# Requests for tiles of sums moved ahead of the shift stores, 32 late sums moved into layer 1's output projection, a third modulation buffer in the recurrence

## The chip, the cores and the metric

The kernel runs on one core of a Trainium2 chip. The metric is the time of one execution on the device, in microseconds (us). Before the change the median of three runs is 3972.62 us (3971.62 to 3973.78).

## What is computed

Two transformer blocks on 256 latent tokens and 256 context tokens, D = 2048, all in fp32. The first mixes an RWKV-7 recurrence (16 heads, two directions) with multi-head latent attention and has a gated feed-forward part (FFN) with a convolution; the second has two layers of pooling and differential attention. The change concerns the modulation vectors:

```python
# first block
sh1, sc1, g1, sh2, sc2, g2 = split(silu(c) @ w_ada + b_ada, 6)
h = rms_norm(x) * (1 + sc1) + sh1
... recurrence, attention, merge, w_out ...
x = x + g1 * rms_norm(out);  x = x + g2 * rms_norm(conv_ffn(...))
# second block, for layer l = 0, 1 (update_ctx only for l = 0)
shift, scale, gate = split(silu(c_2) @ w_ada_2[l] + b_ada_2[l], 3)
shift_c, scale_c, gate_c = split(silu(c_ctx_2) @ w_ada_2[l] + b_ada_2[l], 3)
h = rms_norm_2(x) * (1 + scale) + shift;  p = h @ w_in_2[l]
x = x + gate * (merge(...) @ w_out_2[l])
```

## The kernel before

**The chunks.** Every large product is cut into rounds of (mostly) 16 chunks. A chunk is 128 rows by 512 columns of a weight matrix. SyncE loads two chunks per DMA (512 KB) into `raw`, a ring of four pairs. ScalarE rounds a chunk to `whi` (line 1593), VectorE makes the rest `wlo` (`lo`, line 2238), and TensorE multiplies in three passes (line 891). `whi` and `wlo` have four slots, and VectorE runs three chunks ahead (`LA = 3`). The rounds come in this order: ckv, kpe, cq, mla, kv (4 rounds), r (2), lora, gl, the recurrence (8 iterations, in the code `rwkv`), gate (8), rproj (4 of 8 chunks), mproj (4), wout (4), the FFN (a first pass of 32 chunks, ten of 48, a last one of 16), and then for each layer l of the second block poolv (2), qkva (48 chunks), poolg (2), qkvb (48 chunks), attng (2) and out (4). The text writes qkva0 for l = 0 and qkva1 for l = 1 (the second block's second layer); "layer 1" of the second block in the change's name is l = 0, "layer 2" is l = 1. In layer 2 most chunks are multiplied with 256 columns of activations, those of keys and values with 512.

**The sums.** Part of the modulation is computed on VectorE, not on TensorE: 416 sums, each a product of a tile of the transposed weights (128 x 1024 values, 512 KB) with the condition vector, added up along the row (`reduced`, line 2254) and read from the accumulator. They stand between the chunks' `wlo`, spread by constants: `RED_KV` in each of kv's rounds 2 to 4, `RED_R` in r's, `RED_LORA`, `RED_GATE`, `RED_MPROJ`, `RED_WOUT`, `RED_FFN`, and `RED_VALUES`, `RED_A`, `RED_B`, `RED_C` in the second block. `red_done` counts them. Numbers 0 to 63 have a tile each, through three buffers `red_own`; 64 to 383 come in pairs, two sums to a tile, through two buffers; the last 32 (384 to 415) have a tile each again. These are half rows of the 16 blocks of layer 2's gate, and `RED_C` puts them into qkva1: 2, 20 and 10 in its three groups of 16 chunks.

**Pool's queue.** Pool (GpSimd) issues the tiles' DMAs and all other loads and stores that aren't weights, one after the other, with its waits in program order. `reduce_own(m0, m1)` asks for tiles m0 to m1 - 1 of the first 64, and waits for sum m - 3 before tile m; `reduce_in` (line 694) does so for the others. In kv's rounds 2 to 4, r's two and lora (the loop over `p_`, lines 718 to 738) Pool waits for each of four shifted blocks (`sh_done`), stores it, waits till all four stores have landed (`sh_st`), frees `sh_out` (`sh_free`), in the first pass stores `cond_keep` (2 MB), and then asks for the next tiles. DMAs of all queues share the same 16 DMA engines.

**The recurrence.** In each of its 8 iterations TensorE also multiplies one column tile of `w_ada` (16 x 128 rows by 512 columns) in 8 halves of 512 KB (`ada_half`, line 861, and `ada_mm`, line 857). They go through `ADA_RAW = 2` buffers `ada_raw`; `ada_used` counts the halves used, and Pool (line 700) asks for the next when its buffer is free. The first two of an iteration are asked for at the end of the one before. They stand in TensorE's program between the solves, the chunk steps (lines 1225 to 1229), the chunk outputs (1236 to 1241) and the first state steps (1338); VectorE makes `g1t` and `hd` (2658, 2659) from the chunk steps.

**The order around the late sums.** In the second block Pool reloads `cond_c` (1 MB, the condition vector) and the last 32 tiles in layer 2, after `pw` has landed; VectorE waits for `cond_c` at the start of qkva1 and for `red_done` 416 before the output projection of layer 2. In layer 1's output projection (`out_add`, line 3089) VectorE splits `mix` between the chunks of the first round; `cond_c` lies in `mix`.

**Other loads in Pool's queue.** `oT` (2 MB) is reloaded in the gate rounds (line 801), `x1` (2 MB, line 806) after the last split of `oT`, which is in rproj's last round. Before the change Pool comes to this load only after the request for the tile of sums 116 and 117, and this request waits for sum 113, which stands in mproj's first round.

## Time and profile before

| | before |
|---|---|
| median of 3 runs | 3972.62 us |
| profiled execution | 3977.09 us, span 3975.4 us |
| TensorE matmul busy | 3721.8 us (94%) |
| TensorE weight load busy | 3199.8 us (80%) |
| VectorE busy | 2688.7 us (68%) |
| ScalarE busy | 1724.4 us (43%) |
| DMA | 667.54 MB, mean 168 GB/s |
| mean granted TensorE clock | 0.975 of full speed |

How to read it: the page has the busy time of each engine, the chain of work that ended last, followed back from the last instruction, and the costliest groups of instructions. A busy share is an average over stages with different limits, so the rows below are taken stage by stage. In windows of the span the columns are: from and to, length, then for each engine its busy time and number of instructions, then the granted clock, the mean share of the 16 DMA engines and what they moved. PE is TensorE, PEld its weight load, DVE VectorE, ACT ScalarE, SP SyncE.

### The profile page before, as it was taken

Reading aid. Unit: us, or ns where it says so; the run is one execution under the profiler, and the core shown is the slowest. Engines: PE = TensorE matmul, PEld = TensorE weight load, DVE = VectorE, ACT = ScalarE, POOL = GpSimd, SP = SyncE. Lnnn points to the kernel's source line nnn. Section 1 sums busy time; section 2 is a strip of 40 time slices with the busy share of each in tenths; the row PEclk is TensorE's granted clock in tenths of the full one; section 3 lists DMA queues with packets and bytes.
Section 4 is the critical chain, followed back from the end, with each engine's and each line's share of the span. In section 5 each row is a group of like instructions: output and inputs, shape, how many; then the busy total and the mean of one; then the engine's idle time right before and its main releaser. Section 6 shows DMA issues by size and latency. Waiting matters only on the chain.

```text
span 3975.4 us, 84227 instructions
## 1 busy us (share of the span) xinstructions
PE 3721.8 (94%) x34998; PEld 3199.8 (80%) x34998; DVE 2688.7 (68%) x4743; ACT 1724.4 (43%) x3140; POOL 252.0 (6%) x441
## 2 busy tenths in 40 slices
PE   6999999788888999989999999899999999899999
PEld 2788778666666999989999999887777778777879
DVE  2544477766666786888888888767666643767375
ACT  2544323534344454455444444542433442524354
POOL 0000021111111000000000000000000000010000
PEclk7999999899999999999999999999999999999999
DMA  9422588231322786756777677545235133573336
GB/s 372 151 80 62 206 284 262 78 99 56 100 63 82 240 270 218 240 168 212 233 221 241 217 233 230 193 154 181 74 127 163 60 131 96 162 231 117 117 101 191
DMA packets 290011, 667.54 MB, mean 168 GB/s; under 512 B 21152, under 2 KB 31392, under 8 KB 287600
## 3 DMA queue, kind: packets, MB, share of 16 engines
q1 hardware_dynamic: 233392, 441.73, 34.6%
q0 software_dynamic: 56256, 220.58, 17.6%
q8 instruction: 275, 4.51, 0.5%
q14 instruction: 88, 0.72, 0.1%
HBM read 644.40 MB, written 17.83 MB: 167 GB/s over the span
## 4 chain that ended last, share of the span: by engine, by line
PE 73%; DVE 10%; DMA 9%; issue 4%; ACT 3%; SPq 0%; POOL 0%; POOLq 0%; DVEq 0%; ACTq 0%
PE psum L891 57%; DMA red_own<-in_w_adaT 2%; DVE wlo L2238 2%; PE psum L1153 2%; DMA red_a<-in_w_adaT 2%; DMA ada_head<-in_w_ada 1%; PE psum L1203 1%; DMA ada_raw<-in_w_ada 1%; PE psum L857 1%; PE psum L916 1%; ACT whi L1593 1%; DVE junk_l L2254 1%; DMA red_raw<-in_w_adaT 1%; PE psum L1084 1%; DVE smx L3038 1%
## 5 line engine op out<-in xcount | busy, mean ns | idle before, releaser
L1593 ACT ACTIVATE whi<-raw 128x512 fp32r<-128x512 f32 (+3 forms) x1568 | 970.7, 623 | 1469.3 <-PE psum L891 1425.9
L2238 DVE TENSOR_TENSOR wlo<-raw,whi 128x512 fp32r<-128x512 f32 (+3 forms) x1568 | 1042.2, 680 | 737.3 <-ACT whi L1593 726.5
L891 PE MATMUL psum<-hhi,whi 128*128 128x512 f32 (+1 forms) x2416 | 835.9, 346 | 55.9 <-DVE wlo L2238 27.2
L891 PE MATMUL psum<-hlo,whi 128*128 128x512 f32 (+1 forms) x2416 | 814.3, 337 | 0.0
L891 PE MATMUL psum<-hhi,wlo 128*128 128x512 f32 (+1 forms) x2416 | 814.1, 337 | 0.0
L891 PEld LDWEIGHTS psum<-hhi,whi 128*128 128x128 f32 x2416 | 462.9, 192 | 158.5 <-DVE wlo L2238 58.0
L891 PEld LDWEIGHTS psum<-hhi,wlo 128*128 128x128 f32 x2416 | 462.9, 192 | 48.1
L891 PEld LDWEIGHTS psum<-hlo,whi 128*128 128x128 f32 x2416 | 463.5, 192 | 46.5 <-issue 2.2
L891 PE MATMUL psum<-fhi,whi 128*128 128x256 f32 x1408 | 402.6, 286 | 12.9 <-DVE wlo L2238 8.3
L891 PE MATMUL psum<-flo,whi 128*128 128x256 f32 x1408 | 400.7, 285 | 0.0
L891 PE MATMUL psum<-fhi,wlo 128*128 128x256 f32 x1408 | 400.7, 285 | 0.0
L891 PEld LDWEIGHTS psum<-fhi,whi 128*128 128x128 f32 x1408 | 272.5, 194 | 16.4 <-DVE wlo L2238 11.5
L891 PEld LDWEIGHTS psum<-flo,whi 128*128 128x128 f32 x1408 | 272.7, 194 | 0.0
L891 PEld LDWEIGHTS psum<-fhi,wlo 128*128 128x128 f32 x1408 | 272.6, 194 | 0.0
L891 PE MATMUL psum<-uhi,whi 128*128 128x256 f32 x704 | 201.4, 286 | 2.8 <-DVE ulo L2836 2.8
L891 PE MATMUL psum<-ulo,whi 128*128 128x256 f32 x704 | 200.1, 284 | 0.0
L891 PE MATMUL psum<-uhi,wlo 128*128 128x256 f32 x704 | 200.1, 284 | 0.0
L891 PE MATMUL psum<-mixhi,whi 128*128 128x512 f32 (+1 forms) x512 | 174.3, 341 | 5.6 <-ACT stmp L2198 3.9
L891 PE MATMUL psum<-mixlo,whi 128*128 128x512 f32 (+1 forms) x512 | 172.8, 338 | 0.0
L891 PE MATMUL psum<-mixhi,wlo 128*128 128x512 f32 (+1 forms) x512 | 172.8, 337 | 0.0
L891 PEld LDWEIGHTS psum<-uhi,whi 128*128 128x128 f32 x704 | 136.2, 193 | 4.4 <-DVE ulo L2836 3.0
L2254 DVE CUSTOM_DVE_ANT_0 junk_l<-red_raw,cond_l,mod 128x1024 f32<-128x1024 f32 x106 | 134.6, 1280 | 7.5 <-DMA red_raw<-in_w_adaT 7.5
(459 smaller groups left out, 6950.2 us busy)
## 6 DMA issues: line engine op xcount, KB each, us to landing
raw<-in_w_in SPq DMA_DIRECT2D x328, 512.0 KB, 4.3
red_raw<-in_w_adaT POOLq DMA_DIRECT2D x115, 512.0 KB, 5.2
raw<-in_w_out SPq DMA_DIRECT2D x96, 512.0 KB, 3.8
raw<-in_w_gate SPq DMA_DIRECT2D x88, 512.0 KB, 5.1
raw<-in_w_val SPq DMA_DIRECT2D x88, 512.0 KB, 4.3
raw<-in_w_down SPq DMA_DIRECT2D x88, 512.0 KB, 5.3
ada_head<-in_w_ada SPq DMA_DIRECT2D x64, 512.0 KB, 10.3
red_own<-in_w_adaT POOLq DMA_DIRECT2D x64, 512.0 KB, 6.2
```

What stands on the lines that cost most here:

```text
L857: mm = pe.matmul(PS[4][t:t + 32, 0:256], sc[:, 2 * kh + kk, :], src[:, kk, nh * 256:nh * 256 + 256], start=(kh == 0), stop=(kh == 7), tile ...
L891: mm = pe.matmul(dst, l, r, start=(k == 0 and i == 0 and first), stop=(k == nch - 1 and i == 2), skip_group_check=True)
L916: pe.matmul(PS[bank][:, 0:src.shape[-1]], ones, src, start=(j == 0), stop=(j == of - 1)).then_inc(n_mm, 1)
L1084: done(pe.matmul(PS[5 + j % 2][:, :], lw2[0:LORA, j, :], (wl if j < 2 else al)[0:LORA, j % 2, :], start=True, stop=True), step)
L1153: return pe.matmul(PS[2 * d][HS[1 - e if l == 1 else e], ch(g)], aT[d][HS[1 - e], g, :], xinv[d][HS[1 - e], g, :], start=True, stop=True)
L1203: mx = pe.matmul(PS[2 * d][HS[1 - e], ch(g)], yinv[d][at_(e), g, :], bm[d][at_(e), g, :], start=True, stop=True)
L1593: act.activation(whi[:, lc % HL, 0:width], raw[:, (lc // 2) % RAW, lc % 2, 0:width], ACT.Copy).then_inc(w_hi, 1)
L2238: dve.tensor_tensor(wlo[:, lc % HL, 0:width], raw[:, (lc // 2) % RAW, lc % 2, 0:width], whi[:, lc % HL, 0:width].bitcast(F32), ALU.subtrac ...
L2254: dve.tensor_tensor_reduce(junk[n % len(junk)], (red_own[m % 3] if n < RED_OWN else raw_[m % 2])[:, :], cond[j][:, half], 1.0, acc if m % ...
L3038: own.then(dve.reduce_max(smx2[:, s:s + 2], psum[:, 4:6, 0:nk], axis=AX.X))
```

## The change

1. `reduce_own` asks for all tiles of the round's sums right after the fourth shift store is issued, ahead of the wait for the stores, of `sh_free` and, in the first pass, of the store of `cond_keep`. kv's rounds have 15 sums each for 16, lora 13 for 10.
2. `ADA_RAW` is 3. The third buffer lies at 60.5 KB, where `red_own`'s third buffer and `junk_1` lie. The waits are written for a number of buffers that doesn't divide 8.
3. The 32 last sums stand in rounds 2 to 4 of layer 1's output projection (`out0`), 11, 11 and 10, and use the buffers `red_raw`. Pool loads `cond_c` there, after `x2_in` and the last split of `mix`; VectorE waits for it before the second round. In layer 2 they are gone, with their waits; what reads the modulation of layer 2 waits for all sums.
4. rproj's rounds get one sum each, mproj's five for four, the FFN's ten passes 121 in all for 133, qkva0 12, 22 and 10 for 10, 20 and 10.

```diff
-ADA_RAW = 2
+ADA_RAW = 3
-RED_KV, RED_R, RED_LORA, RED_GATE, RED_MPROJ, RED_WOUT = 16, 3, 10, 7, 4, 8
+RED_KV, RED_R, RED_LORA, RED_GATE, RED_RPROJ, RED_MPROJ, RED_WOUT = 15, 3, 13, 7, 1, 5, 8
-RED_VALUES, RED_A, RED_B, RED_C = 8, (10, 20, 10), (21, 21, 0), (2, 20, 10)
+RED_VALUES, RED_A, RED_B, RED_C = 8, (12, 22, 10), (21, 21, 0), (0, 11, 11, 10)
...
-        ada_raw = [sb(f"ada_raw{i}", [P, 2, N], kb) for i, kb in enumerate((32, 36))]
+        ada_raw = [sb(f"ada_raw{i}", [P, 2, N], kb) for i, kb in enumerate((32, 36, 60.5))]
...
-                    pool.wait_ge(ada_used, 8 * ADA_PAIR * it + c - ADA_RAW + 1 + 8 * ADA_HEAD)
+                    before = c - ADA_RAW if c >= ADA_RAW else next(k for k in range(7, 0, -1) if k % ADA_RAW == c) - 8
+                    pool.wait_ge(ada_used, 8 * it + before + 1 + 8 * ADA_HEAD)
...
                         pool.dma_start(rkv[p_ * 4 - 16 + m, :, TOK:T2], sh_out[:, m, 0:TOK]).then_inc(sh_st[m], 16)
+                reduce_own(n_red, base + n)
+                n_red = max(n_red, base + n)
                 for m in range(4):
                     pool.wait_ge(sh_st[m], p_ * 16 + 16)
...
-            reduce_in(RED_EARLY + 4 + 2 * RED_GATE, RED_EARLY + 7 * RED_GATE + 4)
+            reduce_in(RED_EARLY + 4 + 2 * RED_GATE, RED_EARLY + 7 * RED_GATE + 3)
             pool.wait_ge(o_in, 16)
+            reduce_in(RED_EARLY + 7 * RED_GATE + 3, RED_EARLY + 7 * RED_GATE + 6)
...
-            reduce_in(RED_EARLY + 7 * RED_GATE + 4, RED_LATE)
+            reduce_in(RED_EARLY + 7 * RED_GATE + 6, RED_LATE)
...
-                else:
-                    pool.dma_start(cond_c[:, :], cond_keep[:, 0, :]).then_inc(cond_in3, 16)
-                    reduce_in(RED_BOTH, RED_ALL, red_a)
-                    pool.wait_ge(cond_in3, 48)
                 pool.wait_ge(at_dve[l], 2 * len(AT_DVE[l]))
                 if l == 0:
                     pool.dma_start(xall[:, :, :], x2_keep).then_inc(x2_in, 16)
                     pool.wait_ge(x2_in, 16)
+                    pool.wait_ge(s_lo, 24)
+                    pool.dma_start(cond_c[:, :], cond_keep[:, 0, :]).then_inc(cond_in3, 16)
+                    reduce_in(RED_BOTH, RED_ALL)
+                    pool.wait_ge(cond_in3, 48)
...
                     split_lo(oT, ohi, olo, (2 * it + j + 6) % 8, 2)
+                    if j:
+                        reduced(lo_reduced.n, both_of(cond_l), [junk_1[:, :]])
+                        lo_reduced.n += 1
...
                     c = C0[f"out{l}"] + it * 16
+                    if l == 0 and it == 1:
+                        dve.wait_ge(cond_in3, 48)
                     for i in range(13 + ahead):
...
                         lo(c, (LA + i,))
+                        for _ in range((i + 1) * RED_C[it] // 16 - i * RED_C[it] // 16 if l == 0 else 0):
+                            reduced(lo_reduced.n, [cond_c[:, :]], [junk_1[:, :]])
+                            lo_reduced.n += 1
```

## Rows read from the trace of the kernel before

**Rows 1.** The page: chain that ended last, by line; costliest groups, `whi` and `wlo`.

```profile
PE psum L891 57%; DMA red_own<-in_w_adaT 2%; DVE wlo L2238 2%; PE psum L1153 2%; DMA red_a<-in_w_adaT 2%; DMA ada_head<-in_w_ada 1%; PE psum L1203 1%; DMA ada_raw<-in_w_ada 1%; PE psum L857 1%; PE psum L916 1%; ACT whi L1593 1%; DVE junk_l L2254 1%; DMA red_raw<-in_w_adaT 1%; PE psum L1084 1%; DVE smx L3038 1%
...
L1593 ACT ACTIVATE whi<-raw 128x512 fp32r<-128x512 f32 (+3 forms) x1568 | 970.7, 623 | 1469.3 <-PE psum L891 1425.9
L2238 DVE TENSOR_TENSOR wlo<-raw,whi 128x512 fp32r<-128x512 f32 (+3 forms) x1568 | 1042.2, 680 | 737.3 <-ACT whi L1593 726.5
```

**Rows 2.** Windows: kv's rounds 2 to 4, r's two, out0's second.

```profile
451.35:509.65 58.30, 53.13 (x225) 42.86 (x223) 32.79 (x51) 22.78 (x31) 9.05 (x17) 0.97 0.80 281
509.65:559.10 49.45, 44.01 (x182) 34.88 (x183) 38.75 (x63) 9.16 (x16) 11.17 (x21) 0.97 0.82 273
559.10:605.95 46.85, 45.17 (x196) 36.10 (x195) 37.27 (x61) 12.84 (x21) 10.64 (x20) 1.00 0.88 293
605.95:632.45 26.50, 23.07 (x174) 21.50 (x173) 23.67 (x40) 11.22 (x19) 5.28 (x10) 1.00 0.88 300
632.45:655.50 23.05, 23.05 (x194) 23.05 (x194) 19.03 (x34) 11.14 (x20) 3.90 (x8) 1.00 0.87 284
...
3251.15:3295.35 44.20, 44.20 (x193) 35.73 (x192) 15.70 (x26) 12.19 (x20) 0.00 (x0) 1.00 0.32 95
```

**Rows 3.** Windows: qkva1's first 16 and last 32 chunks, qkvb1's last 32.

```profile
3462.15:3488.75 26.60, 26.60 (x211) 26.10 (x210) 22.44 (x44) 11.14 (x21) 0.53 (x1) 1.00 0.55 165
3488.75:3601.85 113.10, 99.67 (x428) 76.69 (x427) 72.26 (x124) 27.92 (x50) 15.33 (x29) 0.97 0.66 215
...
3701.50:3791.65 90.15, 90.15 (x411) 71.95 (x410) 33.46 (x57) 28.37 (x50) 0.00 (x0) 1.00 0.33 100
```

**Rows 4.** Waits in the recurrence, 720 to 1330: total us, times, longest.

```profile
PE psum L857 <- DMA ada_raw<-in_w_ada: 13.6, 18, 2.4
```

**Rows 5.** Timeline of POOL in kv's second and third rounds: start us, us, instruction.

```profile
471.63 0.54 POOL L725 DMA_DIRECT2D rkv<-sh_out  x1 [2.95 <-DVE sh_out L2431]
...
475.33 1.58 POOL L692 DMA_DIRECT2D red_own<-in_w_adaT  x3
...
549.11 1.57 POOL L692 DMA_DIRECT2D red_own<-in_w_adaT  x3 [5.54 <-DVE mod L2254]
```

**Rows 6.** Timeline of DVE there: sum 2 and sum 15.

```profile
485.22 1.28 DVE L2254 CUSTOM_DVE_ANT_0 junk_e<-red_own,cond_e,vec 128x1024 f32<-128x1024 f32 x1 [8.74 <-DMA red_own<-in_w_adaT]
...
519.22 1.28 DVE L2254 CUSTOM_DVE_ANT_0 junk_e<-red_own,cond_e,mod 128x1024 f32<-128x1024 f32 x1 [3.80 <-DMA red_own<-in_w_adaT]
```

**Rows 7.** Line 692, tiles asked for between 480 and 620.

```profile
DMA to landing us min/median/max: 3.6/6.3/8.2
```

**Rows 8.** Timeline of PE in the second iteration: an `ada_raw` half, the chunk step.

```profile
867.46 0.64 PE L857 MATMUL psum<-ada_raw,sc 128*32 128x256 f32 x8 [1.34 <-DMA ada_raw<-in_w_ada]
...
870.55 0.34 PE L1225 MATMUL psum<-b_tok,wu 64*64 64x64 f32 x8
```

**Rows 9.** Timeline of DVE in the same stretch.

```profile
868.47 0.69 DVE L2659 TENSOR_TENSOR hd<-psum,dec 128x512 f32<-128x512 f32 x1
...
872.73 0.69 DVE L2658 TENSOR_TENSOR g1t<-psum,con 128x512 f32<-128x512 f32 x1 [2.05 <-PE psum L1229]
```

**Rows 10.** Line 698 in qkva1, 3480 to 3600: who waited (us, times), landing.

```profile
  DVE junk L2254: 37.3, 25
...
DMA to landing us min/median/max: 3.7/4.6/7.0
```

**Rows 11.** Timeline of DVE in out0's first round: the last split of `mix`.

```profile
3246.68 1.22 DVE L2733 TENSOR_TENSOR mixlo<-mix,mixhi 128x1024 fp32r<-128x1024 f32 x1 [0.26 <-ACT mixhi L1942]
```

**Rows 12.** Timeline of POOL in mproj: the load of `x1`.

```profile
1552.17 1.18 POOL L806 DMA_DIRECT2D x<-in_xT  x1
```

**Rows 13.** Windows: mproj's second round, an FFN pass, qkva0's first 16 chunks.

```profile
1559.90:1588.35 28.45, 25.03 (x195) 24.62 (x194) 19.72 (x34) 10.83 (x17) 1.60 (x3) 0.94 0.78 254
...
2232.00:2306.00 74.00, 71.71 (x578) 70.80 (x576) 60.32 (x113) 34.59 (x61) 3.60 (x8) 0.98 0.71 223
...
2659.35:2710.00 50.65, 50.65 (x211) 39.27 (x210) 42.45 (x65) 12.39 (x20) 2.77 (x6) 1.00 0.45 138
```

More of the change, by code:

```diff
@@ L80 @@
 RED_FIRST = 8
-RED_KV, RED_R, RED_LORA, RED_GATE, RED_MPROJ, RED_WOUT = 16, 3, 10, 7, 4, 8
+RED_KV, RED_R, RED_LORA, RED_GATE, RED_RPROJ, RED_MPROJ, RED_WOUT = 15, 3, 13, 7, 1, 5, 8
 RED_EARLY = 3 * RED_KV + 2 * RED_R + RED_LORA
-RED_PROJ = RED_EARLY + 7 * RED_GATE + 4 * RED_MPROJ
+RED_PROJ = RED_EARLY + 7 * RED_GATE + 4 * RED_RPROJ + 4 * RED_MPROJ
 RED_MID = RED_PROJ + 4 * RED_WOUT
@@ L862, in ada_half @@
                 c = 8 * j + kh
-                pe.wait_ge(ada_in[c % ADA_RAW], (it * 8 * ADA_PAIR // ADA_RAW + c // ADA_RAW + 1) * 16)
+                pe.wait_ge(ada_in[c % ADA_RAW], (it * len(range(c % ADA_RAW, 8, ADA_RAW)) + c // ADA_RAW + 1) * 16)
                 if kh == 0:
@@ L2141, in heads @@
                             hi(c, range(48, 48 + LA))
-                        if it == 0 and i == 2:
-                            act.wait_ge(red_done, (RED_TURN, RED_ALL)[l])
+                        if l == 0 and it == 0 and i == 2:
+                            act.wait_ge(red_done, RED_TURN)
                         for m in range(4):
@@ L2770, in _ @@
                     lo(c, (i,))
-                    if i % 2:
+                    if i % 2 or i == 8:
                         reduced(lo_reduced.n, both_of(cond_l), [junk_1[:, :]])
@@ L2889, in _ @@
                 if l == 1:
-                    dve.wait_ge(red_done, RED_BOTH)
+                    dve.wait_ge(red_done, RED_ALL)
                 gains(mod2, 48 * l + 16, V("norm_2", 16 * l, 16))
@@ L2957, in late @@
                             reduced(lo_reduced.n, both_of(cond_a), [junk_1[:, :]], red_a)
-                        elif lo_reduced.n < RED_BOTH:
+                        else:
                             reduced(lo_reduced.n, [cond_b[:, :], cond_a[:, 1, :]], [junk_1[:, :]], red_b)
-                        else:
-                            reduced(lo_reduced.n, [cond_c[:, :]], [junk_1[:, :]], red_a)
                         lo_reduced.n += 1
@@ L2966, in heads @@
                     c = C0[f"qkv{'ab'[it]}{l}"]
-                    late_n = (RED_A, RED_B)[it] if l == 0 else (RED_C, (0, 0, 0))[it]
+                    late_n = (RED_A, RED_B)[it] if l == 0 else (0, 0, 0)
                     def ropes(bs):
@@ L2977, in ropes @@
                             done(TT(qk[:, b, TOK:T2], rope2[:, 0, :], rope2[:, 1, :], ALU.add), f"t{b}", it)
-                    if l != it:
-                        dve.wait_ge(cond_in3, 32 + 16 * l)
+                    if l == 0 and it:
+                        dve.wait_ge(cond_in3, 32)
                     for i in range(16):
@@ L3084, in _ @@
                 dve.wait_ge(sg_done, 16 * l + 16)
-                if l:
-                    dve.wait_ge(red_done, RED_ALL)
                 def out_add(it, ahead):
                     c = C0[f"out{l}"] + it * 16
+                    if l == 0 and it == 1:
+                        dve.wait_ge(cond_in3, 48)
                     for i in range(13 + ahead):
```

## The prediction

> **What bounds the kernel now.** I read the page first: 57% of the chain that ended last is line 891, the matmuls of the weight chunks [rows 1], and TensorE is busy for 94% of the span. So most of the kernel stands at TensorE's own pace, and the change can't move that. What it can move are stages in which something else sets the pace. To find them I cut the span where VectorE makes `wlo` of a round's first chunk (16 such instructions are one round of 16 chunks) and compared each round with a quiet one of the same shape. A quiet round over 512 columns takes 44.20 us (the window from 3251.15), over 256 columns 23.05 (from 632.45) [rows 2]. Against these, kv's second, third and fourth rounds take 58.30, 49.45 and 46.85 and r's first 26.50 [rows 2]: 181.10 us where 3 x 44.20 + 23.05 = 155.65 would do, 25.4 us too many. Layer 2's stage qkva1 takes 113.10 us for its last 32 chunks, its twin qkvb1, with the same matmuls and no sums, 90.15 [rows 3]. In the recurrence TensorE waits for `ada_raw` [rows 4]. These three places hold what the change can win. (The timed runs can tell a change from none from about 0.2%, 8 us, on.)
>
> **Part 1, tiles ahead of the shift stores.** In kv's second round Pool stores four shifted blocks (the last is issued at 471.63), waits till they have landed, issues the 2 MB store of `cond_keep`, and only then, from 475.33 on, asks for tiles 2 to 4 [rows 5]. VectorE sits idle for 8.74 us before sum 2, until 485.22 [rows 6]. With the change tile 2 is asked for right behind the store, at 471.63 + 0.54 = 472.2. Tiles here land 6.3 us after issue in the median, 3.6 at best [rows 7]; without the 2 MB store ahead of it I take 5, so sum 2 starts at about 477, 8 us earlier. From there the sums run at the tiles' pace: sum 2 at 485.22, sum 15 at 519.22 [rows 6], 34.0 / 13 = 2.6 us each. Sum 14, now the round's last, starts at 477 + 12 x 2.6 = 508. At TensorE's pace VectorE would be there at 451.35 + 44.2 + 2 x 2.76 + 0.7 = about 502 (2.76 is 44.2 / 16); it is 6 us late. Its lead is three chunks, 8.3 us, less the 1.3 us that a chunk's `whi` and `wlo` take [rows 1], so 7.0: nearly covered. The `cond_keep` store moves to about 503 and costs the tiles there: 2 MB is four tiles' worth of traffic, some 4 us. Lateness peaks at about 10 us, 3 of them uncovered. After that 15 sums in 44.2 us ask for 2.95 us each, slower than the 2.6 that the tiles can do, so it shrinks again.
> In the third and fourth rounds the wait for the stores goes (tiles are asked for only at 549.11, after 5.54 us without anything on Pool [rows 5]; the fourth round has a second such place): 5.25 + 2.65 us. r's first round has a trouble of its own, four shifts in eight chunks of 1.44 us, for which I leave 1.5 of its 3.45 us. Left over the ideal are 3 + 1.5, and about 3 for time at the lower clock (0.97 in two of the rounds [rows 2]) and small misses: 7.5. **Gain 25.4 - 7.5 = 18 us.** Ends: 10, if the tiles' pace rises to 2.9 us as TensorE runs faster; 24, if hardly anything stays.
> What waits behind the moved requests: Pool now sits in the tiles' waits until the round's sum 11 is done, and `sh_free`, which lets the next round's shifts write `sh_out`, comes only after that. That is at chunk 13 or so; the next shift comes at chunk 1 of the next round, over 8 us later: nothing. lora gets 13 sums for 10, each 1.28 us [rows 6]: 4 us more over 16 chunks, still fewer than kv's rounds hold: nothing.
>
> **Part 2, three buffers in the recurrence.** Each of 8 iterations takes the 8 halves of a tile through two buffers, all towards its end. A half can be asked for only once the one two before it is used. TensorE's matmuls wait 13.6 us in 18 places for this, 2.4 at most [rows 4], 1.7 us an iteration. With three buffers each half has the time of one more use as lead, and those stand about 2.5 us apart, so these waits go. What is late next? In the second iteration the half at 867.46 waited 1.34 us [rows 8]. Without this wait the chunk outputs behind it come 1.3 us earlier; the chunk step after them, which started at 870.55 [rows 8], needs `hd` of VectorE, ready at 868.47 + 0.69 = 869.16 [rows 9], so it can start 1.3 us earlier too; and VectorE's 2.05 us of waiting for this step, which ended at 872.73 [rows 9], shrink with it. This wait is passed on whole. The later and shorter ones fall partly into waits of the state steps for VectorE. I take two thirds of 13.6: **gain 9 us.** Ends: 3, if VectorE's chain takes the place, and 14, all of it. The third buffer lies where a buffer of the early sums and the scrap tile of the late ones lie, both unused then.
>
> **Part 3, the 32 late sums.** In qkva1's last 32 chunks 30 sums take a 512 KB tile each through two buffers: 113.10 us where the twin needs 90.15 [rows 3]. VectorE isn't full (72.26 of 113.10); it waits for tiles 25 times, 37.3 us in all [rows 10]. Without the sums these chunks take the twin's time: 22.95 less. The first 16 (26.60, against 23.05 for a quiet round) keep the pool windows and lose 2 sums. **I take 22.5**; ends 18 and 26.
> The sums go into the last three rounds of layer 1's output projection, 11, 11 and 10. Such a round has VectorE busy for 15.70 of 44.20 us [rows 2]; 11 x 1.3 = 14 more fit. Tiles: one each 4.0 us through two buffers, so that a tile may take 8.0 - 1.6 = 6.4 us to land before it paces VectorE. The traffic would be 95 GB/s [rows 2] + 11 x 0.524 MB / 44.2 us = 225 GB/s, near the 215 of qkva1 [rows 3], where tiles landed in 4.6 us in the median [rows 10]. VectorE's new wait for `cond_c`: it is asked for when the last split is done, 3246.68 + 1.22 = 3247.9 [rows 11], is 1 MB, and is there some 8 us later, 3256. VectorE comes to this wait when TensorE has ended the round, three chunks after 3251, at about 3259, and has added its four blocks. Behind it stand the chunks' `wlo`, with three chunks of lead. Nothing, or up to 3 us if the load comes late.
>
> **Part 4, the regrouping.** One sum now stands in each round of rproj. Pool therefore gets earlier through the tile that stood just ahead of the 2 MB load of `x1` at 1552.17 [rows 12]; this load then starts at about 1530, in rproj's last round, and without a tile beside it. The round in which it lay takes 28.45 us [rows 13] against 23.05. The contention with the weights moves there and is a fifth smaller: **gain 2**, ends 0 and 4. The FFN's ten passes get 121 sums for 133. Such a pass of 48 chunks would take 3 x 23.05 = 69.2; the worst takes 74.00 with clock 0.98 [rows 13], where weights and tiles land together. A tenth fewer tiles: **gain 1**, ends -4 and 6, since it may change which pass is hit. qkva0 gets 4 more sums: in its first 16 chunks VectorE has 42.45 us of 50.65 [rows 13], with two more 45: nothing, a loss of 2 us at most.
>
> **The sum.** 18 + 9 + 22.5 + 2 + 1 = 52.5 us. The profiled execution took 3977.1 (span 3975.4), 4.5 above the median of the runs: 3977.1 - 52.5 = 3924.6, and for the median 3972.6 - 52.5 = **3920**.
>
> **Rivals.**
> A. The early rounds are bound by the DMA engines, not by who asks when. For it: share 0.88 and 293 GB/s in the fourth round [rows 2]; in 44.2 us it needs 15 tiles, 8 chunk pairs and 4 stores, (23 x 0.524 + 1.05) MB / 44.2 us = 296 GB/s. Against: 300 GB/s in r's first round [rows 2], and the stalls follow a visible wait of Pool. The gain there would be 8 to 10: 3929. The Trainium skill, in "DMA: Bandwidth & Descriptors" (Specifications), puts a core's share of HBM at about 358 GB/s, which would leave room; no row here shows that much over such a round.
> B. In the recurrence VectorE's chain takes the waits' place and the gain is 0 to 3: 3928. For it: the state steps alternate between the two engines. Against: rows 8 and 9.
> C. Slower than before: the sums carry their price with them. If tiles land in 12 us in the output projection, a sum takes (12 + 1.6) / 2 = 6.8 us, 32 of them 218 us in 132.6: +85, against 52.5 won elsewhere: 4005. It begins at 6.4 us of landing and turns the sign at about 10. Against: 4.6 us at like traffic [rows 10].
> D. qkva1 is slow for its place, not for its sums; then 22.5 goes and 3943 stays. Against: its 25 waits for tiles [rows 10].
> On the price of a tile, a rule speaks against much gain from asking earlier: the Trainium skill, "DMA: Bandwidth & Descriptors" (Anatomy of one DMA), fits 2.0 us + bytes / 436 GB/s to a DMA of this queue, an estimate of 3.2 us for a tile, with which buffers would hardly run dry. The trace disagrees, with 6.3 us [rows 7], and decides.
>
> **How the numbers follow.** Forecast 0.70, A 0.11, B 0.12, C 0.02, D 0.05. The terms' ends reach from 24 to 74 us of gain; they won't all stand at one end, and I take 36 to 68. With A and B inside, 3904 to 3939 should hold 8 in 10. Faster 0.96, same 0.02, slower 0.02.
>
> **What would show it.** With windows cut as here: the four early rounds at 163 us together, VectorE's wait before sum 2 under 2 us; TensorE's waits for `ada_raw` near 0 and each iteration about 1.1 us shorter; qkva1's last 32 chunks at 90 to 91; the output projection still at 44.2 a round; mproj's second round near 24. Wrong, if tiles take over 8 us in the early rounds, if the recurrence keeps its period, or if a round of the output projection grows.

## The result, and the profile after

The changed kernel takes 3918.89 us (median of four runs, 3916.01 to 3922.04); the kernel before, run beside it, 3972.19 (3971.62 to 3973.78). The ratio is 0.9865, 95% interval 0.9848 to 0.9882: 53.3 us less, where 52.5 was forecast. The profiled execution took 3922.04 us (span 3920.4), so the two spans differ by 55.0 us.

First the page of the changed kernel, the lines that answer to [rows 1]. Weight matmuls are now line 895 (891 before), `whi` 1597, `wlo` 2242, the sums 2258, the early tiles' requests 692, the others' 698.

```profile
span 3920.4 us, 84227 instructions
...
PE psum L895 63%; DMA red_own<-in_w_adaT 2%; PE psum L1157 2%; DMA ada_head<-in_w_ada 1%; DVE wlo L2242 1%; PE psum L1207 1%; PE psum L861 1%; PE psum L920 1%; ACT whi L1597 1%; PE psum L1088 1%; DVE smx L3043 1%; PE psum L1222 1%; PE psum L998 1%; PE psum L982 1%; PE psum L983 1%
...
L2242 DVE TENSOR_TENSOR wlo<-raw,whi 128x512 fp32r<-128x512 f32 (+3 forms) x1568 | 1042.7, 680 | 730.6 <-ACT whi L1597 718.8
```

Line 895 now has 63% of the chain that ended last, up from 57% [rows 1]. The work itself hasn't changed: 84227 instructions, and VectorE's `wlo` takes 680 ns as before. Stages that were paced by something else are now paced by TensorE.

The windows of the changed kernel, cut at the same places as [rows 2], [rows 3] and [rows 13]: kv's rounds 2 to 4, r's two, mproj's second, out0's second to fourth, qkva1's first 16 and last 32 chunks, qkvb1's last 32. Columns as before.

```profile
451.10:500.85 49.75, 49.75 (x221) 41.22 (x220) 31.65 (x49) 20.86 (x28) 8.02 (x15) 1.00 0.78 268
500.85:551.15 50.30, 45.90 (x190) 35.93 (x189) 37.25 (x61) 11.53 (x19) 11.19 (x21) 0.97 0.89 309
551.15:594.20 43.05, 43.05 (x192) 35.66 (x191) 36.27 (x61) 11.93 (x21) 10.14 (x19) 1.00 0.89 305
594.20:620.85 26.65, 23.60 (x176) 21.95 (x175) 23.72 (x40) 11.72 (x19) 5.38 (x10) 1.00 0.88 302
620.85:643.90 23.05, 23.05 (x194) 23.05 (x193) 19.04 (x35) 11.14 (x20) 3.81 (x7) 1.00 0.87 284
1540.05:1562.75 22.70, 22.70 (x191) 22.59 (x190) 20.55 (x36) 10.65 (x17) 1.58 (x3) 1.00 0.78 247
3211.50:3255.75 44.25, 44.25 (x194) 35.73 (x193) 25.34 (x42) 12.21 (x20) 4.23 (x8) 1.00 0.69 228
3255.75:3301.80 46.05, 44.42 (x194) 35.75 (x193) 30.24 (x51) 12.20 (x20) 5.81 (x11) 1.00 0.68 216
3301.80:3347.25 45.45, 44.39 (x193) 35.72 (x192) 30.21 (x50) 12.20 (x20) 5.81 (x11) 1.00 0.65 209
3426.65:3453.15 26.50, 26.50 (x210) 26.08 (x210) 21.51 (x43) 11.13 (x20) 0.00 (x0) 1.00 0.50 148
3453.15:3545.05 91.90, 91.90 (x419) 73.49 (x418) 34.76 (x61) 27.27 (x49) 0.00 (x0) 1.00 0.33 103
3646.45:3736.65 90.20, 90.20 (x411) 72.02 (x410) 33.49 (x57) 28.56 (x50) 0.00 (x0) 1.00 0.32 99
```

The four early rounds (kv's second to fourth and r's first) take 169.75 us together, for 181.10. qkva1's last 32 chunks take 91.90 for 113.10 and now stand beside their twin's 90.20. out0's second round has kept its 44.2; the third and fourth have grown by 1.8 and 1.3, with clock 1.00 and TensorE idle for 1.6 and 1.1 us of them. This was not forecast.

Cut into stages in the same way, the span gives this (us; FFN includes the first half of the stage behind it, "layer 2 in" is qkva1 and the pool round behind it). The four single parts of the next section stand beside it. Each column is one profile:

| stage | before | after | part 1 | part 2 | part 3 | part 4 |
|---|---|---|---|---|---|---|
| early rounds | 181.1 | 169.7 | 173.1 | 181.6 | 181.6 | 179.5 |
| recurrence | 607.3 | 598.4 | 608.1 | 597.1 | 603.9 | 602.0 |
| rproj, mproj, wout | 242.8 | 237.6 | 241.1 | 239.9 | 239.7 | 237.6 |
| FFN | 880.0 | 866.5 | 877.7 | 881.0 | 879.6 | 870.1 |
| out0 | 178.7 | 181.9 | 178.7 | 178.7 | 181.4 | 178.8 |
| layer 2 in | 182.5 | 163.1 | 182.3 | 183.1 | 163.0 | 184.3 |
| median of the runs | 3972.2 | 3918.9 | 3967.6 | 3965.2 | 3956.5 | 3952.0 |

So the gains in the pair of profiles are 11.4 + 8.9 + 5.2 + 13.5 - 3.2 + 19.4 = 55.2 us, within 0.2 of the 55.0.

One pair of profiles doesn't give a stage's price well. Every run of the next section has a profile too, and in many of them the code of a stage is the same as before, or as in the changed kernel. These stand together here (us: lowest to highest, mean, in brackets the number of profiles):

| stage | code as before | code as in the change | difference of the means |
|---|---|---|---|
| early rounds | 179.5 to 181.6, 180.9 (4) | 166.1 to 169.7, 167.7 (4) | 13.2 |
| recurrence | 602.0 to 608.1, 605.3 (4) | 596.1 to 605.5, 599.6 (10) | 5.7 |
| rproj, mproj, wout | 239.7 to 242.8, 240.9 (4) | 237.6 to 239.1, 237.9 (10) | 3.0 |
| FFN | 877.7 to 881.0, 879.6 (4) | 864.6 to 870.1, 867.5 (6) | 12.0 |
| out0 | 178.7 to 178.8, 178.7 (4) | 181.4 to 183.0, 181.9 (7) | -3.1 |
| layer 2 in | 182.3 to 184.3, 183.0 (4) | 163.0 to 163.1, 163.0 (10) | 20.0 |

They add up to 50.8 us. So a gain read from the one pair of profiles is off by some 2 us in the early rounds, the merge (rproj, mproj, wout) and the FFN, and by some 3 in the recurrence.

### The profile page after: what moved, and what is told of

It reads as the page before. It is cut to its first block, busy times and chain, and to the rows that moved or that the text cites. A ratio compares the mean times of both kernels' runs of the same rounds, so it can differ in the third digit from the quotient of the medians.

```text
span 3920.4 us, 84227 instructions
## 1 busy us (share of the span) xinstructions
PE 3703.3 (94%) x34998; PEld 3192.7 (81%) x34998; DVE 2688.3 (69%) x4743; ACT 1723.9 (44%) x3140; POOL 251.9 (6%) x441
## 4 chain that ended last, share of the span: by engine, by line
PE 79%; DVE 10%; DMA 4%; issue 3%; ACT 3%; SPq 0%; POOL 0%; DVEq 0%; ACTq 0%; POOLq 0%
PE psum L895 63%; DMA red_own<-in_w_adaT 2%; PE psum L1157 2%; DMA ada_head<-in_w_ada 1%; DVE wlo L2242 1%; PE psum L1207 1%; PE psum L861 1%; PE psum L920 1%; ACT whi L1597 1%; PE psum L1088 1%; DVE smx L3043 1%; PE psum L1222 1%; PE psum L998 1%; PE psum L982 1%; PE psum L983 1%
## 5 line engine op out<-in xcount | busy, mean ns | idle before, releaser
L698 POOL DMA_DIRECT2D red_raw<-in_w_adaT x145 | 76.6, 529 | 1216.4 <-DVE mod L2258 1194.8
```

Source lines behind the costliest of these rows:

```text
L698: pool.dma_start(bufs[m % 2][:, :], A["w_adaT"][m // 2 * P:m // 2 * P + P, m % 2 * HALF:m % 2 * HALF + HALF]).then_inc(red_in[m % 2], 16)
```

## The experiments

**The four parts alone.** Each is the kernel before with one numbered part of the change. The edit of each is that part of the diff shown ahead of the prediction; for part 1 it is

```diff
+                reduce_own(n_red, base + n)
+                n_red = max(n_red, base + n)
                 for m in range(4):
                     pool.wait_ge(sh_st[m], p_ * 16 + 16)
```

with the counts of sums left at 16 a round.

> The kernel before with the requests for tiles moved ahead of the wait for the shift stores, and nothing else (kv's rounds keep 16 sums each, lora 10). Theory: the wait of Pool behind the stores is what the early rounds lose; the four rounds (kv 2 to 4 and r 1, 181.1 us together before) fall to 170 to 173 and the kernel to about 3962. Rival A (the DMA engines bound these rounds and the one sum less per round made the difference): they stay above 177, the kernel above 3968.

Measured: 3967.56 us, ratio 0.999 (0.9979 to 1.0002). Of the stages only the early rounds moved clearly, 181.1 to 173.1, 8.0 us. Asking earlier is worth less than half of the 18 us forecast for it as long as a round has 16 sums; with 15 (the change) it is 11.4.

Part 2 alone, the third buffer with its waits:

```diff
-ADA_RAW = 2
+ADA_RAW = 3
```

> The kernel before with three modulation buffers in the recurrence, and nothing else. Theory: the waits for the tiles go and two thirds of them are won: the recurrence falls by 9 us, the kernel to about 3963. Rival B (VectorE's chain takes their place, and what the changed kernel won there came with the other edits): 0 to 3 us.

Measured: 3965.23, ratio 0.9983 (0.9974 to 0.9993). The waits for `ada_raw` are gone. These windows hold the recurrence in before, after and part 2 alone:

```profile
718.70:1326.00 607.30, 506.23 (x14440) 394.01 (x14440) 408.42 (x716) 252.07 (x452) 85.59 (x132) 0.93 0.27 80
```

```profile
707.10:1305.50 598.40, 508.08 (x14440) 396.39 (x14439) 408.34 (x716) 252.04 (x452) 85.89 (x132) 0.92 0.27 81
```

```profile
719.10:1316.20 597.10, 502.82 (x14440) 391.74 (x14439) 408.24 (x717) 252.08 (x452) 85.90 (x132) 0.93 0.27 82
```

The same 14440 matmuls are busy for 506.2, 508.1 and 502.8 us, with clock 0.92 to 0.93: that part of the stage differs between profiles without any change to it. What the buffers change is the rest, in which TensorE isn't busy: 101.1, 90.3 and 94.3 us.

Part 3 alone, the 32 late sums, with the load of `cond_c` in layer 1:

```diff
-RED_VALUES, RED_A, RED_B, RED_C = 8, (10, 20, 10), (21, 21, 0), (2, 20, 10)
+RED_VALUES, RED_A, RED_B, RED_C = 8, (10, 20, 10), (21, 21, 0), (0, 11, 11, 10)
```

> The kernel before with the 32 late sums moved from qkva1 into the output projection of the second block's first layer, and nothing else. Theory: qkva1 with the stage behind it wins 19 to 20 us; rounds 3 and 4 of the output projection and the norm behind them lose about 4 as in the changed kernel, since a sum stands just ahead of the round's last blocks: the kernel at about 3957. Rival (the loss in the projection comes from tiles landing late because of what the other edits moved): the projection keeps 44.2 us a round and the kernel is at 3953.

Measured: 3956.5, ratio 0.9966 (0.9954 to 0.9978), 16.2 us. Layer 2's stage gives 19.5, the output projection takes 2.7 back (181.4 for 178.7), and the stage between them 0.9.

Part 4 alone, the regrouping:

```diff
-RED_KV, RED_R, RED_LORA, RED_GATE, RED_MPROJ, RED_WOUT = 16, 3, 10, 7, 4, 8
-RED_VALUES, RED_A, RED_B, RED_C = 8, (10, 20, 10), (21, 21, 0), (2, 20, 10)
+RED_KV, RED_R, RED_LORA, RED_GATE, RED_RPROJ, RED_MPROJ, RED_WOUT = 16, 3, 10, 7, 1, 5, 8
+RED_VALUES, RED_A, RED_B, RED_C = 8, (12, 22, 10), (21, 21, 0), (2, 20, 10)
```

> The kernel before with one sum in each round of rproj, five in mproj's, and so 121 for 133 in the FFN's ten passes and 4 more in qkva0, and nothing else (the early rounds keep their numbers). Theory: the FFN's passes lose time where a burst of three sums stands between chunks; with 12 sums a pass there are none and the ten passes fall from 706 to 695 us, mproj and wout by 5: the kernel at about 3956. Rival (the passes' stalls are accidents of phase, which any shift of time moves elsewhere): the passes stay at 700 or more and the kernel at 3963 or more.

Measured: 3952.02, ratio 0.9956 (0.9939 to 0.9972), 20.7 us by the medians; in its profile the stages of the merge give 5.2 and the FFN 9.9. The part for which 3 us were forecast is the largest of the four.

Beside these four the kernel before had a median of 3972.72 us. Their gains by the medians are 5.2 + 7.5 + 16.2 + 20.7 = 49.6 us, against 53.3 for all together: they add up within the scatter of such differences.

**The store of `cond_keep`.** On the changed kernel, the store goes from the loop's first pass (kv's second round) to its fifth, the end of r's second round. Pool then issues it at 638.34, so that its traffic lies in lora, which keeps its 40.3 us:

```diff
-                if p_ == 0:
+                if p_ == 4:
```

> The changed kernel with the 2 MB store of cond_keep issued in r's second round instead of kv's second. Theory: this store is what is left of the early loss, since it lands beside three tiles and the weights (they took 13 us instead of 6): the four early rounds fall from 169.8 to 162 to 165 us, lora loses at most 1, and the kernel is at about 3913. Rival A (the DMA engines' pace through all of kv's rounds): they stay at 168 or more and the kernel at 3918.

Measured: 3914.30 us (3905.52 to 3923.62), ratio 0.9848 (0.9824 to 0.9872). The early rounds take 165.5 us for 169.7, 4.2 less. But the size isn't settled by this pair: three later kernels with the same early rounds as the changed one took 166.1, 167.0 and 167.9, and the one other kernel with the store moved and 15 sums took 162.3 ("Together"). By the means, 163.9 for 167.7, the store costs 3.8, and the two groups are only 0.6 apart at their ends. What it does in the changed kernel is in the timeline. Pool, then VectorE, then TensorE:

```profile
503.04 0.53 POOL L692 DMA_DIRECT2D red_own<-in_w_adaT  x1 [1.27 <-DVE mod L2258]
503.70 0.54 POOL L736 DMA_DIRECT2D cond_keep<-cond_e  x1
504.85 0.53 POOL L692 DMA_DIRECT2D red_own<-in_w_adaT  x1 [0.61 <-DVE mod L2258]
```

```profile
511.13 1.29 DVE L2258 CUSTOM_DVE_ANT_0 junk_e<-red_own,cond_e,vec 128x1024 f32<-128x1024 f32 x1 [4.29 <-DMA red_own<-in_w_adaT]
...
518.45 1.29 DVE L2258 CUSTOM_DVE_ANT_0 junk_e<-red_own,cond_e,mod 128x1024 f32<-128x1024 f32 x1 [2.91 <-DMA red_own<-in_w_adaT]
```

```profile
513.09 0.50 PE L895 MATMUL psum<-hhi,whi 128*128 128x512 f32 x1 [2.90 <-DVE wlo L2242]
...
514.07 0.63 PE L895 MATMUL psum<-hhi,whi 128*128 128x512 f32 x1
514.50 0.63 PE L895 MATMUL psum<-hlo,whi 128*128 128x512 f32 x1
```

The tiles asked for on both sides of the store are late by 4.29 and 2.91 us for VectorE, the first of these stops TensorE for 2.90 us, and from 514.07 on its matmuls follow one another every 0.43 us, where it had been 0.23. The window shows the granted clock there, 0.50, the lower of the clock's two levels (1.2 for 2.4 GHz):

```profile
514.00:517.00 3.00, 3.00 (x8) 2.30 (x7) 1.47 (x3) 0.00 (x0) 0.55 (x1) 0.50 0.98 402
```

**The last sum of a round.** On the changed kernel, the sums of an output projection's round are spread over 15 chunks for 16, so that none stands behind the last chunk:

```diff
-for _ in range((i + 1) * RED_C[it] // 16 - i * RED_C[it] // 16 if l == 0 else 0):
+for _ in range(min(i + 1, 15) * RED_C[it] // 15 - min(i, 15) * RED_C[it] // 15 if l == 0 else 0):
```

> The changed kernel with the late sums of each output projection round spread over its first 15 chunks, none behind the last. Theory: the sum behind the last chunk delays VectorE's additions that free PSUM; without it rounds 3 and 4 fall from 46.0 and 45.5 to 44.2, the norm behind them from 51.7 to 50.7, the kernel to about 3915. Rival (the traffic of the tiles slows the projection): rounds 3 and 4 stay above 45.

Measured: 3916.16 us, ratio 0.9848 (0.9832 to 0.9865); the difference to the changed kernel is within the scatter of the medians, but the stage shows it: 179.1 us for 181.9, its rounds 44.2, 44.2 and 44.6. TensorE's waits in it, first in the changed kernel, then here (us in total, times, longest):

```profile
PE psum L895 <- DVE xall L3115: 2.7, 2, 1.6
```

```profile
PE psum L895 <- DVE xall L3115: 0.2, 1, 0.2
```

**The FFN's count and its bursts.** Undo only the FFN's and qkva0's part of the regrouping on the changed kernel:

```diff
-RED_VALUES, RED_A, RED_B, RED_C = 8, (12, 22, 10), (21, 21, 0), (0, 11, 11, 10)
+RED_VALUES, RED_A, RED_B, RED_C = 8, (10, 22, 0), (21, 21, 0), (0, 11, 11, 10)
```

The FFN gets what the second block doesn't: 133 sums.

> The changed kernel with 133 sums again in the FFN's ten passes and 12 fewer in qkva0 (10, 22 and 0), nothing else. Theory: the bursts of three sums come back and the ten passes go from 695 to 706 us, the kernel to 3929; the passes with 14 sums (the fourth, seventh and tenth) are the slowest. Rival (the gain there came from the sums' shift against the tiles' pairs, or from what lies ahead): the passes stay below 698, the kernel at 3919.

Measured: 3928.16 us, ratio 0.9886 (0.9869 to 0.9902), 9 us slower than the changed kernel by the medians. Its ten passes take 700.2 us for 695.1, with the ends 8.0 more. The theory had 706 for the passes, the rival less than 698: neither came true. With the same 133 sums in the same bursts the kernel before took 706.1 (705.9 to 708.7 in its four profiles). So the number of sums explains 5.0 of the 11.0 us; the other 6.0 came with other edits. Part 4 alone has 9.7 of the 11.0. Which edit it is, no run separates.

Why should a tenth fewer sums give even 5 us? In a pass two of the three groups of 16 chunks make sums, each in three bursts. With 121 sums all bursts but one are of two, with 133 thirteen are of three. The next kernel keeps the 133 and spreads them singly:

```diff
-                for i in range(4):
-                    lo(c, range(lc0 + 4 * i + LA, lc0 + 4 * i + 4 + LA))
-                    for _ in range((i + 1) * n // 3 - i * n // 3 if i < 3 else 0):
+                for i in range(16):
+                    lo(c, (lc0 + i + LA,))
+                    for _ in range((i - 2) * n // 12 - (i - 3) * n // 12 if 3 <= i < 15 else 0):
```

> The changed kernel with 133 sums in the FFN as in the run before this one on the FFN, but spread one by one over the chunks instead of in bursts of two and three. Bursts are the cause: the ten passes at 693 to 696 us. The number of sums is: 699 to 706.

Measured: 3921.02 us, ratio 0.9868 (0.9839 to 0.9897). The ten passes in before, after, with 133 sums, and with 133 spread. These windows run from TensorE's first matmul of the passes to its last, not from `wlo` to `wlo`, since in the spread kernel VectorE is ahead of TensorE by another amount:

```profile
1813.67:2517.96 704.29, 698.22 (x5762) 693.89 (x5760) 595.41 (x1107) 343.33 (x600) 34.35 (x65) 1.00 0.72 228
```

```profile
1786.36:2479.65 693.29, 693.29 (x5762) 691.66 (x5760) 582.70 (x1083) 342.75 (x600) 31.20 (x59) 1.00 0.72 227
```

```profile
1784.56:2482.84 698.28, 696.55 (x5761) 692.36 (x5760) 595.21 (x1107) 343.38 (x600) 34.52 (x65) 1.00 0.73 230
```

```profile
1782.32:2478.26 695.94, 694.09 (x5762) 691.86 (x5760) 597.21 (x1105) 341.29 (x600) 34.34 (x65) 1.00 0.74 231
```

The changed kernel's passes hold no idle time of TensorE at all. With the bursts taken apart, 133 sums take 695.94 us, 2.3 of the 5.0 us less, at the same traffic. (Cut at `wlo` it is 696.05 for 700.15, which makes it 4.1: more than TensorE gained.) TensorE's idle time is as long as with the bursts, 1.85 and 1.73 us; what is shorter is its matmuls' time. So about half of the count's 5.0 us goes with the bursts, by one profile of each, and the rest with the count. The worst pass of before [rows 13] shows what a burst of three does. Pool, VectorE, TensorE:

```profile
2248.50 0.53 POOL L698 DMA_DIRECT2D red_raw<-in_w_adaT  x1 [4.29 <-DVE mod L2254]
```

```profile
2251.43 1.28 DVE L2254 CUSTOM_DVE_ANT_0 junk_l<-red_raw,cond_l,vec 128x1024 f32<-128x1024 f32 x1
2252.63 1.28 DVE L2254 CUSTOM_DVE_ANT_0 junk_l<-red_raw,cond_l,vec 128x1024 f32<-128x1024 f32 x1
2255.92 1.28 DVE L2254 CUSTOM_DVE_ANT_0 junk_l<-red_raw,cond_l,mod 128x1024 f32<-128x1024 f32 x1 [1.99 <-DMA red_raw<-in_w_adaT]
```

```profile
2257.87 0.39 PE L891 MATMUL psum<-fhi,whi 128*128 128x256 f32 x1 [2.06 <-DVE wlo L2238]
```

The third sum needs a new tile. Pool could ask for it only at 2248.50, when the burst before had freed its buffer; it landed in 7.4 us, VectorE waited 1.99, and the next `wlo` stands behind this sum. Of the 6.0 us that TensorE waits for `wlo` in the ten passes of before, 5.5 are four such places, each right behind a third sum that had waited 0.64 to 1.99 us for its tile. They lie in the third, fourth, seventh and tenth pass; with 133 sums on the changed kernel there are two stops behind a sum's wait for its tile, of 0.40 us (a second sum, in the fourth pass) and 1.18 (a third, in the seventh). The tiles landed in 5.0 us in the median before and in 4.6 there; what made them faster isn't shown.

**What bounds the early rounds.** What keeps the early rounds of the kernel with the store moved, 165.5 and 162.3 us in its two profiles, from less? Two kernels on top of it. In the first the tiles of sums 0 to 63 are loaded by half and read twice (these sums are then not the reference's; all other work is in place):

```diff
-pool.dma_start(red_own[m % 3][:, :], A["w_adaT"][m // 2 * P:m // 2 * P + P, m % 2 * HALF:m % 2 * HALF + HALF]).then_inc(own_in[m % 3], 16)
+pool.dma_start(red_own[m % 3][:, 0:HALF // 2], A["w_adaT"][m // 2 * P:m // 2 * P + P, m % 2 * HALF:m % 2 * HALF + HALF // 2]).then_inc(own_in[m % 3], 16)
...
+twice = red_own[m % 3][:, 0:HALF // 2].unsqueeze(1).to_broadcast([P, 2, HALF // 2])
```

> The kernel with the later store, and the first 64 tiles loaded as half tiles (256 KB) that VectorE reads twice, so that its work stays and their traffic is halved; the 64 sums are not the reference's sums. Rival A, as it stands after the later store (what is left over the ideal in the early rounds, 10 us of 165.5, is the DMA engines' pace): the four rounds fall to about 158, VectorE's waits for these tiles to near 0. Other theory (VectorE's own order of shifts and sums): they stay at 162 to 166. r's first round keeps about 25.5 in both.

In the second the traffic of a tile stays, and a round has one sum less; lora takes the three:

```diff
-RED_KV, RED_R, RED_LORA, RED_GATE, RED_RPROJ, RED_MPROJ, RED_WOUT = 15, 3, 13, 7, 1, 5, 8
+RED_KV, RED_R, RED_LORA, RED_GATE, RED_RPROJ, RED_MPROJ, RED_WOUT = 14, 3, 16, 7, 1, 5, 8
```

> The kernel with the later store, kv's rounds with 14 sums each and lora with 16. If the tiles' pace is what is left: kv's three rounds lose 2 to 4 us more than with 15, lora stays at 40.3, the four early rounds at 161 to 163. If VectorE's order is: 165 as with 15.

Measured: 3914.58 us, 0.9852 (0.9823 to 0.9881), and 3916.41, 0.9857 (0.9827 to 0.9886). The windows over the four early rounds: before, after, store moved, half tiles, 14 sums:

```profile
451.35:632.45 181.10, 165.37 (x773) 135.34 (x772) 132.48 (x212) 56.00 (x84) 36.15 (x68) 0.98 0.84 285
```

```profile
451.10:620.85 169.75, 162.31 (x773) 134.76 (x772) 128.88 (x206) 56.03 (x84) 34.72 (x65) 0.99 0.86 295
```

```profile
450.75:616.30 165.55, 159.91 (x773) 133.82 (x772) 128.87 (x206) 56.05 (x84) 34.32 (x64) 1.00 0.85 289
```

```profile
451.50:609.90 158.40, 157.99 (x773) 133.88 (x772) 128.98 (x207) 56.04 (x84) 34.52 (x64) 1.00 0.69 221
```

```profile
453.60:611.95 158.35, 157.94 (x773) 133.88 (x772) 125.51 (x200) 56.04 (x84) 32.59 (x61) 1.00 0.85 292
```

Both reach the same floor, 158.4 us, in which TensorE is busy but for 0.4 us. The kernel with 14 sums reaches it at 292 GB/s, so the DMA engines carry the load (its tiles landed in 6.6 us in the median, as with 15). A round of kv has room for 14 tiles of that landing time, and not for 15: none of the six profiles with 15 whole tiles reached the floor. With the floor known, each kernel's excess splits in two: time in which TensorE stands still, and time that its 773 matmuls take beyond 157.9 us because the granted clock has dropped. Before: 15.7 + 7.5. After: 7.4 + 4.4. With the store moved: 5.6 + 2.0.

**Together.** First the store moved, the 15 chunks and 119 sums in the FFN:

```diff
-RED_VALUES, RED_A, RED_B, RED_C = 8, (12, 22, 10), (21, 21, 0), (0, 11, 11, 10)
+RED_VALUES, RED_A, RED_B, RED_C = 8, (13, 23, 10), (21, 21, 0), (0, 11, 11, 10)
...
-                if p_ == 0:
+                if p_ == 4:
```

> The changed kernel with the store in r's second round, no sum behind a projection round's last chunk, and 119 sums in the FFN (11 in the first pass, 12 in the others) with qkva0 at 13, 23 and 10. Theory: 6 + 4 + 1 us less than the changed kernel: about 3908. Rival A and the traffic theory: 3916 or more.

Measured: 3915.77 us, ratio 0.9851 (0.9834 to 0.9867). The stages are short (out0 179.4, FFN's ten passes 693.9, early 162.3, where the store's move alone had given 165.5), but the recurrence took 600.9 us, 4.8 more than with the store moved alone, and the median isn't distinguishable from the changed kernel's. Then 14 sums in kv's rounds and 16 in lora as well:

```diff
-RED_KV, RED_R, RED_LORA, RED_GATE, RED_RPROJ, RED_MPROJ, RED_WOUT = 15, 3, 13, 7, 1, 5, 8
+RED_KV, RED_R, RED_LORA, RED_GATE, RED_RPROJ, RED_MPROJ, RED_WOUT = 14, 3, 16, 7, 1, 5, 8
```

> All edits that won in a stage, on the changed kernel: the store of cond_keep in kv's last pass, 14 sums in each of kv's rounds and 16 in lora (the run before it reached 158.4 us in the four early rounds), the output projection's sums over 15 chunks, and 119 sums in the FFN with 4 more in the second block's first stage. Theory (the stages add up, and the rest of a run's time is TensorE's time at the lower clock): early rounds 158 to 160, output projection 179 to 180 for 181.9, FFN's ten passes 693.9 for 695.1, so 11 + 2.5 + 1 = 14 to 15 us less than the changed kernel at the same clock: median 3902 to 3910, ratio 0.983. Rival (what is won early is given back in the recurrence as time at the lower clock, since TensorE idles less before it): the recurrence takes 603 to 606 as in the run before, with TensorE's busy time in it 509 to 511 for 508.1, its idle time still 91 to 95, and the median stays at 3913 to 3918.

Measured: 3906.50 us (3905.45 to 3913.80), ratio 0.9845 (0.9831 to 0.9858), 63.6 us less than before on the same chip, where the change has 53.3. The interval overlaps the changed kernel's, so it is probably, not certainly, the fastest here. Its profiled execution took 3912.29 us, 5.8 above the median: early 158.4, out0 179.0, ten passes 693.9, and the recurrence 602.8:

```profile
697.66:1300.48 602.82, 509.62 (x14440) 397.54 (x14439) 408.40 (x717) 252.10 (x452) 85.92 (x132) 0.92 0.27 81
```

The idle time in it is 93.2 us, as in the others with three buffers; the matmuls take 509.6. The median is in the first theory's range. In this one profile the recurrence has come near the rival's numbers, 4.4 us longer than in the changed kernel's; the early rounds' 11.4, the output projection's 2.9 and the FFN's 1.2 are there all the same.

## Why the prediction was right, and where its steps were off

The median came within 1.1 us of the forecast, but the sum held by luck: by the stages of the pair the terms were 11.4, 8.9, 16.2 and 18.7 us (55.2 in all) for 18, 9, 22.5 and 3. By the means over all profiles they are 13.2, 5.7, 16.9 and 15.0 (50.8).

**Part 1: 18 us forecast, 11.4 measured (13.2 by the means).** The place and the first step hold. Tile 2 was asked for at 471.89 (forecast 472.2), landed in 6.2 us (taken as 5), and the wait before sum 2 fell from 8.74 [rows 6] to 1.92 us:

```profile
471.89 0.54 POOL L692 DMA_DIRECT2D red_own<-in_w_adaT  x1
```

```profile
478.14 1.28 DVE L2258 CUSTOM_DVE_ANT_0 junk_e<-red_own,cond_e,vec 128x1024 f32<-128x1024 f32 x1 [1.92 <-DMA red_own<-in_w_adaT]
```

What failed is "from there the sums run at the tiles' pace: 2.6 us each". From sum 2 to sum 15 they took 518.45 - 478.14 = 40.3 us, 3.1 each. With the store moved away it was 2.8 in one profile and 2.6 in the other, so the pace of [rows 6] was not wrong in itself: it doesn't hold across the store. The second step that failed is the price of the moved store: four tiles' worth of traffic, 3 us of it uncovered, for 4.2 measured in the pair and 3.8 by the means. The third is that the rest, which was to shrink again behind the store, stayed: with the store moved the early rounds are still 3.9 to 7.2 us above the floor. A tile that takes 6.3 us to land [rows 7] and 1.3 to be read comes through three buffers every 2.5 us if nothing else holds it up; against 44.2 / 15 = 2.95 that looked like room, but the runs reach the floor at 44.2 / 14 = 3.16 and not at 2.95. The lower end of the term, 10, had been reckoned for just this case, and nearly came true. The ideal of 155.65 us was 2.7 too low as well: the floor is 158.4.

What was said to wait behind the moved requests, `sh_free` and the next shifts, costs nothing: the kernels with 14 sums and with half tiles keep that order and reach the floor. lora takes 40.3 us with 10, 13 and 16 sums (40.4 in the last kernel).

**Rival A** had two halves. "Bound by the DMA engines" falls with 14 sums at 292 GB/s and the floor. But its number, a gain of 8 to 10, is near the 11.4, and what kept the early rounds off the floor once the store was moved is the pace at which tiles come: half the bytes a tile takes it away, with VectorE's work left as it was, and so does one tile less a round. The landing of the early tiles asked for between 480 and 600, first in the changed kernel, then with half tiles:

```profile
DMA to landing us min/median/max: 4.3/6.3/13.5
```

```profile
DMA to landing us min/median/max: 2.9/3.7/5.5
```

The Trainium skill ("DMA: Bandwidth & Descriptors", Anatomy of one DMA) fits 2.0 us + bytes / 436 GB/s to one DMA of this queue, an estimate of 3.2 us for a whole and 2.6 for half a tile. At 221 GB/s in the rounds the median is 1.1 us above this fit, at 295 GB/s 3.1 above. The fit has no term for other traffic; here the measured landing decides.

**Part 2: 9 us forecast, 8.9 in the pair of profiles, and that agreement is partly luck.** All 13.6 us of waits are gone [rows 4]. But by idle time, which the clock doesn't touch, the four profiles with two buffers have 97.5 to 101.1 us (mean 99.0) and the ten with three have 90.3 to 94.6 (mean 92.7): 6.3 us, 45% of the waits (14.2 in the mean of the four) and not two thirds. In the recurrence of the pair the idle time fell by 10.8 and the busy time grew by 1.9. What takes back the rest is in part VectorE, as rival B had it. In the means over the same profiles the waits for `ada_raw` fall by 13.9 us, those for VectorE's `zs` and `hd` grow by 3.8, and time for which the profile names nothing ("issue") by 3.2, which stays unexplained. In the pair these two rows have grown, the first from 12.3 us, the second from nothing:

```profile
PE psum L1342 <- DVE zs L2678: 13.9, 25, 0.7
...
PE psum L1229 <- DVE hd L2663: 2.0, 5, 0.4
```

**Part 3: 22.5 us forecast, 16.2 measured.** Rival D is out: without its sums qkva1 runs like its twin, 91.90 and 90.20 us. The term was mis-sized in two places. First, the 22.95 us were the difference of two windows that begin and end where VectorE makes a `wlo`. Such a mark runs ahead of TensorE or behind, and 1.8 us that the shorter window had given up came back in the pool round behind it (44.6 for 42.8). A stage should be cut where both kernels have caught up; then it is 19.4. Second, the output projection: the tiles landed in 4.7 us in the median (taken 4.6), `cond_c` in 5.4, and VectorE didn't wait for it. Rival C is out. The wait that did come is another. Sum 394 stood behind the round's last chunk and ahead of the four blocks' additions, which set PSUM free:

```profile
3262.43 1.28 DVE L2258 CUSTOM_DVE_ANT_0 junk<-red_raw,cond_c,vec 128x1024 f32<-128x1024 f32 x1 [0.54 <-DMA red_raw<-in_w_adaT]
3263.64 0.08 DVE L2258 DVE_READ_ACCUMULATOR2_ANT mod<- 128x1 f32 x1
3263.64 0.48 DVE L3114 SCALAR_TENSOR_TENSOR xall<-psum,mod,xall 128x256 f32<-128x256 f32 x1
3264.15 0.48 DVE L3115 SCALAR_TENSOR_TENSOR xall<-psum,mod,xall 128x256 f32<-128x256 f32 x1
```

```profile
3264.78 0.47 PE L895 MATMUL psum<-mixhi,whi 128*128 128x512 f32 x1 [1.63 <-DVE xall L3115]
```

TensorE's next round waits until the first additions have read its block. The prediction had asked what the new wait for `cond_c` holds up, and counted VectorE's busy time, but not what stands behind the last sum in its order. The kernel without a last sum takes 2.8 of the 3.2 us back.

**Part 4: 3 us forecast, 18.7 by the stages of the pair (15.0 by the means), and both of its steps failed.** Of the merge, 5.2 us for 2 in the pair, outside the end of 4; by the means it is 3.0, inside. mproj's second round, 28.45 us in [rows 13], took 25.3 to 26.7 in the three other profiles in which its code is the same. The load of `x1` went to 1519.04, where Pool has no other tile on its way, as forecast, though TensorE had by then begun mproj's first round (at 1518.84) and not rproj's last:

```profile
1508.72 0.53 POOL L698 DMA_DIRECT2D red_raw<-in_w_adaT  x1 [22.25 <-DVE mod L2258]
1519.04 1.18 POOL L810 DMA_DIRECT2D x<-in_xT  x1 [9.79 <-DVE olo L2737]
1530.76 0.54 POOL L698 DMA_DIRECT2D red_raw<-in_w_adaT  x1 [10.54 <-DVE mod L2258]
```

mproj's second round fell from 28.45 us to 22.70. The first grew from 24.3 to 25.5 by the `wlo` marks, but from TensorE's first matmul of it to the first of the next round it takes 23.1 us in every profile, the kernel before too. So the contention didn't move with four fifths of its price: TensorE no longer lost anything to it. That it had been the load and a tile together is argued, not shown: the load itself landed in 15.1 us before and in 11.4 after. Of the FFN, 13.5 us for 1, where the end was 6. "A tenth fewer tiles" reckoned with bytes. Of the ten passes' 11.0 us, 5.0 come back with the 133 sums, some half of them by the bursts; what gives the other 6.0 stays open. The prediction had reckoned the quiet pass at 69.2 us, but priced the worst [rows 13] by its share of traffic and didn't look for what sets it off, a sum that waits for its tile ahead of a `wlo`. qkva0's first 16 chunks didn't grow (50.1 for 50.4).

So the sum held because the misses cancelled: 6.6 and 6.3 too much in parts 1 and 3, 15.7 too little in part 4. Of the terms' own ends the FFN's 6 was passed, and in the pair the merge's 4; the late sums' gain in layer 2 (19.4) is inside its own (18 to 26), and their cost in the output projection (3.2) just outside (0 to 3). The profile signs that were given hold for sum 2, the `ada_raw` waits, the iteration (8.9 / 8 = 1.1 us) and, within 1 us, qkva1; they fail for the early rounds (169.7 for 163), for mproj's second round on the good side, and for the third and fourth rounds of the output projection. That a round of the output projection grows had been named as a sign that the prediction is wrong, and for its cost there it is.

## To carry to other kernels

When work is threaded into an engine's order, look at what stands right behind each piece: a sum ahead of the additions that free PSUM cost 1.3 to 1.8 us a round, and a sum that waits for its tile ahead of a `wlo` up to 2.1 us. Before you price an edit by one stage of two profiles, look at every profile in which that stage's code is the same: here four with the same early rounds spread over 3.6 us, and the store's price is about as large. Cut a stage where the bounding engine begins and ends it, and compare idle time, not stage length, where the clock varies.
